# Attention mask added in the PSUM accumulator and convolution taps dealt out anew, in the first layer type of a two-model kernel

## The reference, cut to what matters

```python
v = a * sigmoid(b)                                   # a, b: two 1024-wide slices of z
y = depthwise_conv(v, dw, width 31) + db             # then layer norm, silu, a gate, @ w_conv_out
...
s = einsum(q, k) * HEAD_DIM ** -0.5                  # 16 query heads, 4 key heads, head width 64
s = where(abs(kpos - qpos) <= 128, s, -1e30)         # the window mask
m = maximum(max(s), sink)
p = exp(s - m);  p = p / (sum(p) + exp(sink - m))
o = p @ v                                            # then a silu gate, @ w_attn_out
...
x + (g0 * y_conv + g1 * y_ret + g2 * y_attn) @ w_out # y_ret: retention, 4 heads
```

## Time and profile before

| | us |
|---|---|
| median of 3 runs | 3243.54 (3242.83 to 3244.89) |
| the profiled execution | 3237.26 |
| its span | 3235.4 |
| TensorE matmul busy | 2975.1 (92%) |
| VectorE busy | 2320.2 (72%) |
| ScalarE busy | 1478.8 (46%) |
| granted TensorE clock, mean | 0.962 of full speed |

### The profile page before, as it was taken

How to read it: one execution, slowest core, us unless ns; L and a number is a source line. 1 busy time by engine, 2 the same in 40 slices (tenths; PEclk the granted TensorE clock), 3 DMA queues, 4 the chain that set the end, 5 groups by cost and what they waited for, 6 DMA issues and landing times. The chain is left out here.

```text
span 3235.4 us, 46193 instructions
## 1 busy us (share of the span) xinstructions
PE 2975.1 (92%) x18054; PEld 2653.8 (82%) x18054; DVE 2320.2 (72%) x4125; ACT 1478.8 (46%) x2274; POOL 425.7 (13%) x250
## 2 busy tenths in 40 slices
PE   6899989888999897999789999998699979999998
PEld 6687777877778676899789988887599979998887
DVE  5868996586899665694986677767479496556665
ACT  3344333334433333445654455554344575444554
POOL 0100000010000000498100000001069600000000
PEclk9999999999999997999999999999799999999999
DMA  6435554543555451455136677774055414555554
GB/s 213 143 130 195 200 184 165 182 159 130 176 201 196 159 178 66 146 175 187 62 112 238 224 244 245 269 265 135 31 172 184 156 46 141 184 178 195 193 192 162
DMA packets 126827, 550.90 MB, mean 170 GB/s; under 512 B 13811, under 2 KB 18068, under 8 KB 102164
## 3 DMA queue, kind: packets, MB, share of 16 engines
q1 hardware_dynamic: 124716, 543.23, 49.4%
q10 hardware_dynamic: 1896, 4.72, 0.6%
HBM read 541.60 MB, written 6.29 MB: 169 GB/s over the span
## 5 line engine op out<-in xcount | busy, mean ns | idle before, releaser
L1913 PE MATMUL e_ps<-k_hhi,q_hi 128*128 128x256 f32 x2304 | 656.8, 285 | 0.1
L1913 PE MATMUL e_ps<-k_hlo,q_hi 128*128 128x256 f32 x2304 | 652.8, 283 | 0.0
L1913 PE MATMUL e_ps<-k_hhi,q_lo 128*128 128x256 f32 x2304 | 652.8, 283 | 0.0
L2193 DVE TENSOR_TENSOR q_lo<-q_raw,q_hi 128x1024 fp32r<-128x1024 f32 x394 | 482.6, 1225 | 187.2 <-ACT q_hi L2002 186.1
L2002 ACT ACTIVATE q_hi<-q_raw 128x1024 fp32r<-128x1024 f32 x538 | 564.1, 1048 | 10.4 <-DMA q_raw<-up 5.9
L735 DVE TENSOR_TENSOR k_wlo<-k_raw,k_whi 128x2048 fp32r<-128x2048 f32 x158 | 360.3, 2286 | 147.1 <-ACT k_whi L565 147.1
L1913 PEld LDWEIGHTS e_ps<-k_hhi,q_hi 128*128 128x128 f32 x2304 | 443.4, 192 | 0.6 <-DVE k_hlo L2220 0.5
L1913 PEld LDWEIGHTS e_ps<-k_hlo,q_hi 128*128 128x128 f32 x2304 | 443.3, 192 | 0.0
L1913 PEld LDWEIGHTS e_ps<-k_hhi,q_lo 128*128 128x128 f32 x2304 | 443.0, 192 | 0.0
L565 ACT ACTIVATE k_whi<-k_raw 128x2048 fp32r<-128x2048 f32 x158 | 300.1, 1910 | 275.5 <-PE f_psA L435 133.8
L1894 POOL TENSOR_TENSOR q_lo<-q_raw,q_hi 128x1024 fp32r<-128x1024 f32 x144 | 368.6, 2572 | 82.3 <-ACT q_hi L2002 82.0
(11 more groups left out here) (349 smaller groups left out, 5126.7 us busy)
## 6 DMA issues: line engine op xcount, KB each, us to landing
k_raw<-ws SPq DMA_DIRECT2D x180, 1024.0 KB, 4.9
q_raw<-down SPq DMA_DIRECT2D x288, 512.0 KB, 3.8
q_raw<-up SPq DMA_DIRECT2D x256, 512.0 KB, 4.3
k_x<-ada SPq DMA_DIRECT2D x48, 512.0 KB, 3.8
e_ada<-ada SPq DMA_DIRECT2D x48, 512.0 KB, 5.3
out<-k_x SPq DMA_DIRECT2D x3, 1024.0 KB, 4.2
k_x<-out SPq DMA_DIRECT2D x3, 1024.0 KB, 6.3
k_x<-x SPq DMA_DIRECT2D x2, 1024.0 KB, 7.0
```

The source lines that it names most:

```text
L1913: last = nc.tensor.matmul(psD(n), w, h, start=kt == 0 and i == 0, stop=kt == KT - 1 and i == 2)
L2193: V.tensor_tensor(lo[:, i % RING, :], raw[:, i % RING, :], hi[:, i % RING, :].bitcast(F32), ALU.subtract).then_inc(S["lo_dve"], 1)
```

## The change

1. The mask is added by TensorE: after each of the four score matmuls (`stop=False`) comes one with the identity as the stationary tile and the mask as the moving one, both rounded to fp32r at the start of the layer by two ScalarE copies.
2. The maximum reads PSUM, and so do the four exponentials; the mask addition on VectorE is gone.
3. In `attn_probs` TensorE issues the transposes of pair j first and the scores of pair j+1 after them. The wait on `s_masked` is gone.
4. The taps: 10 at each `glu_a`, 1 a unit in the heads, 3 a unit in attention and in addition 3 at each `attn_probs` (ahead of the maximum) and 3 at each `attn_values` (ahead of the reciprocals), the rest evenly over the units up to `conv_mean`.

```diff
+    ident_r = pb("f_identr", [P, P], F32R)
+    mask_r = pb("f_maskr", [P, CH], F32R)
...
                         def scores(p):
-                            if p:
-                                pe.wait_ge(S["s_masked"], p)
                             for hh in range(2):
                                 r = slice(64 * hh, 64 * hh + 64)
                                 for t in range(NT):
-                                    last = nc.tensor.matmul(psS[:, hh, t * T:(t + 1) * T], qT[r, p, t * P:(t + 1) * P],
-                                                            kT[r, p // 2, :], start=True, stop=True)
+                                    c = slice(t * T, (t + 1) * T)
+                                    nc.tensor.matmul(psS[:, hh, c], qT[r, p, t * P:(t + 1) * P], kT[r, p // 2, :], start=True, stop=False)
+                                    last = nc.tensor.matmul(psS[:, hh, c], ident_r[:, :], mask_r[:, c], start=False, stop=True)
                             last.then_inc(S["s_ready"], 1)
 
+                        pe.wait_ge(S["mask_ready"], 2)
                         pe.wait_ge(S["small_read"], m_attention)
                         scores(0)
                     elif name == "attn_probs":
 
-                        if j < 7:
-                            scores(j + 1)
                         pe.wait_ge(S["s_exp"], j + 1)
...
                         last.then_inc(S["pt_ready"], 1)
+                        if j < 7:
+                            scores(j + 1)
...
+                act.wait_ge(G["in_co"], 16)
+                nc.scalar.activation(ident_r[:, :], ident[:, :], ACT.Copy).then_inc(S["mask_ready"], 1)
+                nc.scalar.activation(mask_r[:, :], con["mask"], ACT.Copy).then_inc(S["mask_ready"], 1)
...
-                                ins = nc.scalar.activation(row, row, ACT.Exp, bias=NMX[:, c:c + 1], accum_out=SUM[:, c:c + 1])
+                                ins = nc.scalar.activation(row, psS[:, i // 2, (i % 2) * T:(i % 2 + 1) * T], ACT.Exp, bias=NMX[:, c:c + 1], accum_out=SUM[:, c:c + 1])
...
-                tap_share = [0.4 if u_attn0 <= u < u_attn1 else 1.0 for u in range(u_tap0, u_tap1)]
+                def more_taps(count, known=taps_total):
+
+                    tap_goal[0] = min(tap_goal[0] + count, known)
+                    taps(tap_goal[0])
...
                         def masked(p):
                             dve.wait_ge(S["s_ready"], p + 1)
-                            if p >= 2:
-                                dve.wait_ge(S["pt_ready"], p - 1)
-                            mask = con["mask"].rearrange("p (a n) -> p a n", a=1).to_broadcast([P, 2, CH])
-                            V.tensor_tensor(sm[:, p % 2, :].rearrange("p (a n) -> p a n", a=2), psS[:, 0:2, :], mask, ALU.add).then_inc(S["s_masked"], 1)
-                            dve.wait_ge(S["s_masked"], p + 1)
                             nm = NMX[:, 4 * p:4 * p + 4]
-                            own.link(V.tensor_reduce(nm, sm[:, p % 2, :].rearrange("p (a n) -> p a n", n=T), AX.X, ALU.max, negate=True))
+                            own.link(V.tensor_reduce(nm, psS[:, 0:2, :].rearrange("p a (t n) -> p (a t) n", t=NT), AX.X, ALU.max, negate=True))
...
                     elif name == "attn_probs":
+                        more_taps(3)
                         if j < 7:
                             masked(j + 1)
                     elif name == "attn_values":
                         c = slice(4 * j, 4 * j + 4)
+                        more_taps(3)
                         dve.wait_ge(S["s_sink"], j + 1)
...
-                    if s["nu"] and u_tap0 <= s["u"] < u_tap1:
-                        known = 2 * TAPS * (j + 1 if name == "glu_a" else j if name == "glu_b" else 4)
-                        taps(min(known, int(taps_total * sum(tap_share[:s["u"] + s["nu"] - u_tap0]) / sum(tap_share))))
+                    if name == "glu_a":
+                        more_taps(10, 2 * TAPS * (j + 1))
+                    elif s["nu"] and u_heads <= s["u"] < u_attn0:
+                        more_taps(s["nu"])
+                    elif s["nu"] and u_attn0 <= s["u"] < u_attn1:
+                        more_taps(3 * s["nu"])
+                    elif s["nu"] and u_attn1 <= s["u"]:
+                        left = u_late - (s["u"] - u_attn1)
+                        more_taps(-(-(taps_total - tap_goal[0]) * s["nu"] // left) if left > s["nu"] else taps_total)
```

More of the change, by code:

```diff
@@ L299, in first_layer @@
             a_sq a_ss a_rstd a_qn act_hi act_lo conv_y conv_sq conv_sd conv_u conv_t conv_p
-            s_ready s_masked s_negmax s_exp s_sink pt_ready pt_read o_ready m_add ones_ready
+            s_ready mask_ready s_negmax s_exp s_sink pt_ready pt_read o_ready m_add ones_ready
             decay_exp dec_arg dec_ready ro_ready r_var r_rstd r_og m_done x_done in_crow in_ada ada_done""".split()
@@ L509, in _ @@
                     elif name == "attn_act":
-                        pe.wait_ge(S["s_masked"], 8)
                         pe.wait_ge(S["acc_read"], by[("attn_values", 7)]["n"] + 1)
@@ L791, in taps @@
                     tap_next[0] = max(tap_next[0], min(upto, taps_total))
-                u_tap0, u_tap1 = by[("glu_b", 1)]["u"], by[("conv_mean", 0)]["u"]
-                u_attn0, u_attn1 = by[("attn_start", 0)]["u"], by[("attn_act", 0)]["u"]
-                tap_share = [0.4 if u_attn0 <= u < u_attn1 else 1.0 for u in range(u_tap0, u_tap1)]
+                u_heads, u_attn0, u_attn1 = by[("aq", 0)]["u"], by[("attn_start", 0)]["u"], by[("attn_act", 0)]["u"]
+                u_late = by[("conv_mean", 0)]["u"] - u_attn1
+                tap_goal = [0]
+                def more_taps(count, known=taps_total):
+                    tap_goal[0] = min(tap_goal[0] + count, known)
+                    taps(tap_goal[0])
                 bc8 = lambda ap: ap.rearrange("p (o n) -> p o n", o=1).to_broadcast([P, KT, T])
```

## The result

The changed kernel takes 3252.18 us (median of 20 runs, 3244.03 to 3257.17); the kernel before has 3241.61 us over the 20 runs beside it (3231.66 to 3253.3). The ratio is 1.0030, 95% interval 1.0022 to 1.0039: slower by 0.3%, where I had forecast no measurable change, 3241.5 us. The value lies in my range, 0.8 us from its upper end, and in the part above 3250 that I had given 0.20. The profiled execution took 3251.43 us with a span of 3249.6, against 3237.26 and 3235.4 before; the spans differ by 14.2 us, the medians by 10.6.

A forecast was written before the change was run, and what follows sets the result against it. Attention was taken as bound by the loop of VectorE and ScalarE, not TensorE. Per layer 0.35 - 8.0 + 14.0 - 8.1 = -1.75, two layers -3.5, +1.6 in layer 1: -1.9, forecast 3241.5 us, range 3229 to 3253 (8 in 10).

The forecast's parts named there:

- Start of a layer and heads: Before attention, per layer: +0.35 us for two new ScalarE copies; heads -8.0 us from fewer taps, smaller stalls and full clock.
- VectorE's loop in attention: VectorE and ScalarE, mask addition to mask addition: +1.45 us for a pair with one unit, +1.8 with two.
- The rival that the taps are free: Attention: taps fall into VectorE's 4.32 us idle, -11 us instead of +14, 3192 us; chance 0.08 together with half of it, 3216.
- The mask matmuls, priced at 0.114 us each: Attention, TensorE: four matmuls of 256 columns a pair, 0.5 us a pair or 3.7 us a layer, hidden behind the loop.
- The first unit starts 9.8 us after the first scores; before it was 9.7: 0: Start of attention, TensorE: one stand of 3.6 us, then transposes 1.6 and scores 2.9 us at lower clock; no net change.
- The +14.0 for VectorE's loop: Attention stage, per layer: more taps ahead of the maximum lengthen the loop by 14.0 us, bounds +10 and +17.
- 3 to 5 us for the transposes of pairs 3, 5 and 6: Attention, TensorE: it would stand 3 to 5 us during the stage for these pairs' transposes.
- The sum: Whole kernel: -1.75 us per layer, -3.5 for two, +1.6 for one line in layer 1, so -1.9 us.
- Line 383 in layer 1: End of attention, line 381 before the change: +1.6 us in layer 1, as in layer 0 it already runs slow.
- Retention: Per layer -8.1 us: 4.2 from low-part stalls, convolution wait 3.9 where 7.8 were; bounds -4 and -11.
- After `conv_mean`: Rest of the layer behind the convolution's mean: nothing moves, 0 us.
- the one on the slower side: Rival: retention waits for high parts; half given back 3249.5 us, nothing 3258; chance 0.22 with a dearer attention loop in it.

The follow-up runs named there:

- the mask first: Changed kernel with two mask matmuls of 512 columns ahead of the four query-key matmuls, in place of four in turn with them: 3236.68 us, ratio 0.9974.
- both repairs: Changed kernel with two 512-column mask matmuls ahead of the score matmuls and ten taps behind each maximum: 3189.25 us, ratio 0.9835.

## Why the prediction was wrong

- **Start of a layer and heads**: -7.65 us a layer forecast, -7.85 and -8.28 measured, with 0.7 us of waits left where I had said about 1. Right, and the taps alone give it.
- **VectorE's loop in attention**: right to 0.1 us a pair, at both sizes. The mask addition's removal is worth 15.92 - 14.51 = 1.4 us a pair (1.35 forecast), the taps cost 2.8. Its 4.3 us gap stayed, as I had said (4.17). The rival that the taps are free is wrong for where they stand, and right for a place 1.3 us further on, behind the maximum.
- **The mask matmuls, priced at 0.114 us each from rows of one kind, and with them "The first unit starts 9.8 us after the first scores; before it was 9.7: 0"**: this step of the prediction failed. A mask matmul cost 0.65 us at full clock, and the first unit starts 15.7 and 16.7 us after the first scores. Of the 7.6 us in layer 0 about 4 are the alternation at full clock (two blocks of scores at 3.67 instead of 1.7 us). The rest goes with the clock: the eight transposes and the second pair's scores run at a granted 0.50 (the scores forecast at 2.9 us took 6.51), the unit behind them at 0.67, so that it takes 7.97 us (156.69 to 164.66); with four mask matmuls first it was 1.00 and 5.56 us. My price came from units in which every stationary tile has 128 rows; no row of before showed two sizes in one block, and I gave the price no upper bound. The +14.0 for VectorE's loop held: with the mask first the stage takes the 131 us of the forecast. The "3 to 5 us for the transposes of pairs 3, 5 and 6" fell with it: in layer 0 one wait of 1.2 us was left in the change, and three of together 8.8 with the mask first.
- **The sum**: attention came out 7.9 and 6.8 us above the forecast, 14.7 in all. The rest nearly cancels (heads -0.8, ahead of the first unit -1.4, after the first `conv_mean` +0.9, retention +0.5): -1.9 + 14.7 - 0.8 = +12.0 us up to layer 1's `conv_mean` (1058.75 to 1070.77), of the 14.2 between the spans. The other 2.2 I did not trace.
- **Line 383 in layer 1**: 3.68 us instead of 1.94, +1.6 forecast. Right. The wait ahead of it is 6.5 us there and 3.8 in layer 0; the forecast was about 7.
- **Retention**: -8.1 us forecast, -7.6 measured and, without the 1.7 us of line 383, -8.3 in layer 1. The convolution's wait is the forecast 3.9 us; the low parts kept 1.1 of their 4.2.
- **After `conv_mean`**: 0 forecast, +0.9 us in layer 0; the cause is open.
- **The rivals**: the one on the slower side named 3249.5 for a retention that gives back half, "with a dearer attention loop in it". The time was near it, the mechanism was neither: retention gave nearly all, the loop was as forecast, and the dear part was TensorE's scores at the start.

The Trainium skill, "TensorEngine Tiling (Array Packing)", section "Key Properties", says that going from one tiling mode to another, and not just to another tile, drains TensorE. The runs agree: the loads no longer run ahead where the number of rows changes (eight times in a pair of the change, twice in the kernel before), with 0.33 us idle at a step to 128 rows at full clock (0.23 in the kernel with 64-row masks), and they do where it is equal. That the array drains is the page's word; the traces show the loads and the time. Had I weighed that rule, it would have been the rival that came true; the page gives no time for the drain.

## What to carry to other kernels

When a matmul is put between others, compare its tile size with its neighbours': here a mask matmul that changed the number of rows and changed it back cost 0.65 us, and 0.16 when the same matmuls stood grouped by size. Work that is to be hidden goes to the place in the program where its engine stands, and not merely into the stage in which it idles: seven more taps ahead of the maximum cost 2.8 us a pair, ten behind it filled 4.0 us in which the engine had stood anyway. When two bounds lie close together, test the repairs together before giving up either.

## What the runs showed of the hardware

- At full clock the mask matmul of 128 rows and 256 columns costs 0.65 us in turn with 64-row ones and 0.16 in a group of its own; in fp32 and in turn 0.92, (4.74 - 1.07) / 4. With 64 rows, in turn with others of 64, it costs 0.19.
- A maximum of 128 x 1024 took 1218 ns from PSUM and 1220 ns from SBUF; an exponential of 128 x 256 took 473 and 497 ns.
- In the alternated block of the change the weight loads start together with their matmuls, at the step to 128 rows (with 0.33 us of idle time ahead of it) and at the step back to 64. Among equal rows they run ahead, by 0.1 us in the units (176.36 for 176.48).
- The granted clock fell right behind alternated scores though TensorE waited for nothing (0.87 over a pair, 13.61 instead of 12.13 us), not behind each of them: with the fp32 mask, where the alternated block is longest, it was 1.00 from the third scores to the eighth in both layers. In the kernel with both repairs it was 1.00 in a pair of one unit and in one of two. What decides it was not tested.
